# Four of the attention stage's eight modulation blocks computed on VectorE during the mixer's input projection, the other four at half a block per head

## The reference, cut to what matters

```
m_lat = split(silu(c) @ ada_w[i] + ada_b[i], 6)       # ada_w[i]: 2048 x 12288
h = x;  hn = rms_norm(h) * (1 + m_lat[1]) + m_lat[0]
layer 0: p = hn @ w_in                                 # 512 tokens x 6560 columns
         y = [diff_attention(p[:, :3072]), rwkv7(p[:, 3072:])] @ w_out
layer 1: conformer convolution
h = h + m_lat[2] * y                                   # output gate of the mixer
h = h + m_lat[5] * mlp(rms_norm(h) * (1 + m_lat[4]) + m_lat[3])
```

## Time and profile before

| | us |
|---|---|
| median of 3 runs | 3243.42 |
| profiled execution, span from first to last instruction | 3244.1 |
| input projection, from its first matmul to its last copy | 121.8 to 606.5 |
| attention | 606.5 to about 740 |
| TensorE / VectorE / ScalarE busy | 3021.5 / 2202.5 / 1244.9 |

### The profile page before, as it was taken

How to read it: one execution, slowest core, us unless ns; L and a number is a source line. 1 busy time by engine, 2 the same in 40 slices (tenths; PEclk the granted TensorE clock), 3 DMA queues, 4 the chain that set the end, 5 groups by cost and what they waited for, 6 DMA issues and landing times.

```text
span 3244.1 us, 49985 instructions
## 1 busy us (share of the span) xinstructions
PE 3021.5 (93%) x20896; PEld 2496.8 (77%) x20896; DVE 2202.5 (68%) x2736; ACT 1244.9 (38%) x1430; POOL 217.1 (7%) x394
## 2 busy tenths in 40 slices
PE   5899999778889888999999999999889999999999
PEld 2588987536677766788888888799867888888887
DVE  3677766477887885577777878759974555555554
ACT  1322221174444443344443434343643343434342
POOL 1000000001000000012122121100000000000000
PEclk9799999899999998999999999999989999999999
DMA  9976887790000033668888888756205455555553
GB/s 326 352 273 238 317 289 246 271 368 24 12 14 13 22 67 106 208 230 285 279 295 281 293 292 277 260 166 184 92 23 181 159 194 186 191 185 192 194 182 130
DMA packets 306013, 640.59 MB, mean 197 GB/s; under 512 B 19035, under 2 KB 23937, under 8 KB 303585
## 3 DMA queue, kind: packets, MB, share of 16 engines
q1 hardware_dynamic: 269280, 529.94, 48.3%
q0 software_dynamic: 28384, 94.76, 9.0%
q10 hardware_dynamic: 8128, 12.72, 1.1%
HBM read 623.81 MB, written 13.40 MB: 196 GB/s over the span
## 4 chain that ended last, share of the span: by engine, by line
PE 83%; DVE 9%; DMA 4%; issue 2%; ACT 2%; ACTq 0%; SPq 0%; POOLq 0%; DVEq 0%
PE ps L445 46%; PE ps L463 15%; PE ps L465 7%; DMA raw<-in_ada_w_dram 3%; PE ps L2385 2%; PE ps L1662 2%; DVE rw_scl L1336 1%; DVE rw_mb L1353 1%; PE ps L382 1%; PE ps L1820 1%; PE ps L1772 1%; DVE rw_mt L1356 1%; DVE rw_scc L1339 1%; PE ps L1569 1%; DVE line L752 1%
## 5 line engine op out<-in xcount | busy, mean ns | idle before, releaser
L422 DVE TENSOR_TENSOR split_lo<-raw,split_hi 128x2048 fp32r<-128x2048 f32 (+1 forms) x372 | 849.7, 2285 | 496.7 <-ACT split_hi L410 488.8
L410 ACT ACTIVATE split_hi<-raw 128x2048 fp32r<-128x2048 f32 x368 | 702.1, 1911 | 1180.4 <-PE ps L445 840.3
L463 PE MATMUL ps<-xa,split_hi 128*128 128x512 f32 x2048 | 723.4, 398 | 6.4 <-ACT xa L617 6.4
L465 PE MATMUL ps<-xa,split_lo 128*128 128x256 f32 x2048 | 574.0, 280 | 0.0
L463 PEld LDWEIGHTS ps<-xa,split_hi 128*128 128x128 f32 x2048 | 384.6, 188 | 103.0 <-ACT xa L617 7.4
L445 PE MATMUL ps<-split_hi,hT_hi 128*128 128x512 f32 x1024 | 399.6, 390 | 0.0
L445 PE MATMUL ps<-split_hi,hT_lo 128*128 128x512 f32 x1024 | 398.5, 389 | 0.0
L445 PE MATMUL ps<-split_lo,hT_hi 128*128 128x512 f32 x1024 | 398.4, 389 | 0.0
L465 PEld LDWEIGHTS ps<-xa,split_lo 128*128 128x128 f32 x2048 | 386.5, 189 | 0.2
L445 PEld LDWEIGHTS ps<-split_hi,hT_hi 128*128 128x128 f32 x1024 | 192.2, 188 | 41.4 <-issue 1.8
L445 PEld LDWEIGHTS ps<-split_hi,hT_lo 128*128 128x128 f32 x1024 | 192.2, 188 | 40.2
(11 more groups left out here) (386 smaller groups left out, 4521.1 us busy)
## 6 DMA issues: line engine op xcount, KB each, us to landing
raw<-in_mlp_w_dram SPq DMA_DIRECT2D x256, 1024.0 KB, 5.4
raw<-in_ada_w_dram SPq DMA_DIRECT2D x64, 1024.0 KB, 9.6
raw<-in_mix_in_w_dram SPq DMA_DIRECT2D x48, 1024.0 KB, 5.7
raw<-in_conv_pw_w_dram SPq DMA_DIRECT2D x48, 1024.0 KB, 5.4
gate<-in_ada_w_dram SPq DMA_DIRECT2D x172, 256.0 KB, 5.0
line<-in_ada_w_dram POOLq DMA_DIRECT2D x171, 256.0 KB, 5.1
late<-in_ada_w_dram POOLq DMA_DIRECT2D x85, 256.0 KB, 5.0
tmpa<-in_ada_w_dram SPq DMA_DIRECT2D x84, 256.0 KB, 4.9
```

What stands on the lines that cost most here:

```text
L410: nc.scalar.activation(split_hi[:, c, :, 0:n], raw[:, c, :, 0:n], ACT.Copy).then_inc(hi_done, 1)
L422: nc.vector.tensor_tensor(split_lo[:, c, :, 0:n], raw[:, c, :, 0:n], split_hi[:, c, :, 0:n], ALU.subtract).then_inc(lo_done, 1)
L463: pe.matmul(ps[:, base + j, :], split_hi[:, c, kk, j * P:(j + 1) * P], both, start=(k == 0), stop=False, skip_group_check=True)
L465: mm = pe.matmul(ps[:, base + j, 0:SEQ], split_lo[:, c, kk, j * P:(j + 1) * P], xa_hi[:, k, :], start=False, stop=(k == KT - 1), skip_grou ...
```

## The change

The output gate's blocks 8 to 11 are made on VectorE beside the projection (20 blocks, 320 pieces instead of 256), with other rates per item. The attention keeps blocks 12 to 15: two chunks per head, a block over two heads, and a copy and store on ScalarE in every second head. The gate is now stored as one row, so it is read with one DMA instead of four, behind another semaphore.

```diff
-ADA_A, ADA_T = 8, 1
-ADA_M, M_BUF = 16, 6
+ADA_A, ADA_T = 8, 4
+ADA_M, M_BUF = 20, 6
 Q_AT = ADA_A
-Q_ALL = Q_AT + ADA_T * HEADS
+Q_ALL = Q_AT + ADA_T
-        PARTED = [(0, 2), (0, 3)]
+        PARTED = [(0, 3)]
             if n == 0:
-                pool.wait_ge(ada_st, 16 * 4)
+                pool.wait_ge(mrow_st, 16 * ADA_M)
         def mix_ada(b):
-            return (0, (16 + b) * NB) if b < 8 else (1, (b - 8) * NB)
+            if b < 8:
+                return 0, (16 + b) * NB
+            return (1, (b - 8) * NB) if b < 16 else (0, (b - 8) * NB)
-        STEP_RATE = [3, 1, 7, 4, 4, 8, 3, 3, 7, 7, 7, 8, 8]
+        STEP_RATE = [3, 1, 8, 6, 6, 9, 8, 8, 8, 8, 9, 9, 0]
             gate_bias(pool, 0, 2)
-            for g in range(4):
+            for g in range(parts_of(0, 2)):
                 gate_part(pool, 0, 0, 2, g)
-            pool.wait_ge(ada_st, 16 * HEADS)
+            pool.wait_ge(ada_st, 16 * ADA_T)
-            with sp.Fori(0, HEADS) as i:
-                q = i + Q_AT
-                send_ada(sp, 0, i * NB + Q_AT * NB, ("ada", q - 1))
+            for i in range(ADA_T):
+                send_ada(sp, 0, (16 - ADA_T + i) * NB, ("ada", Q_AT + i - 1))
-                    if n < HEADS:
-                        act_ada(act, 0, (n + Q_AT) * NB, n + Q_AT, 0, n * 16, 0)
+                    if n < HEADS and n % 2:
+                        i = n // 2
+                        act_ada(act, 0, (16 - ADA_T + i) * NB, i + Q_AT, 0, i * 16, 0)
-            def weights(i, c):
-
+            def weights(n, half):
+
+                i, c = n // 2, 2 * (n % 2) + half
                 pe_ada_chunk(pe, i + Q_AT, i + (Q_AT + MIX_M), c, 0, i + Q_AT)
                     if n < HEADS:
                         weights(n, 0)
-                        weights(n, 1)
                     if n:
                         maps_turned(n - 1)
                     if n < HEADS:
-                        weights(n, 2)
+                        weights(n, 1)
                     if n + 1 < HEADS:
                         turned(n + 1)
-                    if n < HEADS:
-                        weights(n, 3)
```

## The result

The kernel after takes 3271.57 us (median of 4 runs, 3270.39 to 3274.56) against 3244.06 us before (median of 4, 3241.31 to 3245.73): ratio 1.0088, 95% interval 1.0073 to 1.0102. It is slower by 27.5 us; 3260 was forecast, with 3250 to 3270 as the forecast's own range and 3243 to 3277 as the whole one. Its profiled execution has a span of 3268.7 us and took 3270.39 us, so the spans differ by 24.6 us, and the traces have to explain that number. (Wherever both are on record, the time exceeds the span by about 1.7 us, so the span of 3244.1 before fits its run of 3245.73 us, the slowest of the four, while the one after is its fastest: that is the 3 us between the two differences.)

The account below looks back on a forecast made before the run. TensorE was taken as the bound, with 83% of the chain, and VectorE's lead as used up in product 7. Projection +30 and attention -13.3 gave +16.7, 3260 us; own range 3250 to 3270, 8-in-10 range 3243 to 3277.

Parts of the forecast that it names:

- rival 3: Projection: piece waits of 2.0 to 2.3 us in every item, +36 to +44 instead of +30, 3266 to 3274; chance 0.13.
- The item sum: Projection, products 5 to 7: VectorE's split 2.2 us, steps, and piece wait per item, added without pause from 315.3 to 443.8.
- The step that ends the twelfth block: Projection, product 7: VectorE's step at 443.8, needed by the sum before chunk (8,2), which starts 29.6 us later.
- The restart after the last stall: Projection: TensorE restarts slowly after a stall, 1.3 us each; only the last counts, +1.4.
- The small stalls of before: Projection: the stall at 548.82 and a like one in product 12 go, estimated -2 us.
- -0.9 as forecast: Attention: one head's wait for a chunk before its values goes, 0.6 us and part of the chunk's 1.06.
- Heads 0 to 2: Attention: the 6.86 us chunk wait goes and 22.5 us between maxima becomes an ordinary head's 11.9, -10.6.
- "Thus no gain" in an ordinary head: Attention: the 11.9 us chain from one head's values to the next holds no transfer, so nothing is gained.
- rival 2: Attention: 2.7 us gaps drop TensorE to half clock, values 4.0 instead of 2.0 us in eight heads, +16, 3276; chance 0.09.
- Head 6's -1.8: Attention, head 6: the 3.74 us wait stays, but one of two chunks that cost 3.46 us goes, -1.8.
- 4 (it costs nothing): Projection: moved blocks cost TensorE nothing and the attention gains as forecast, -13, 3230; chance 0.06.
- rival 1: VectorE's lead covers products 6 and 7; transfer-paced attention heads speed up to -23.5: net -8.5, 3235; chance 0.12.

Follow-up runs that it names:

- the other rates: Kernel after with the same 320 steps at other rates per product, 4 and 6 in products 6 and 7: 3262.35 us, ratio 1.0051 to the kernel before.
- one buffer more: Kernel after with seven piece buffers instead of six: 3265.81 us, ratio 1.0069 to the kernel before.
- the second table version: Kernel after with ScalarE's square-root wait in every second head moved behind the wait for the next maxima: 3267.70 us, ratio 1.0073 to the kernel before.
- one round of filler: Kernel after, first table edit (no effect in the targeted heads), plus four zero-adding matmuls in heads 1 to 7 before the second half block: 3272.29 us, ratio 1.0077.
- attention alone: Kernel after with the projection's old 16 blocks and rates, blocks 8 to 11 left out: 3241.18 us, ratio 0.998 to the kernel before.
- two rounds: Kernel after with seven buffers, other rates, freed table load, and twice four zero-adding matmuls in heads 1 to 7: 3247.45 us, ratio 1.0007 to the kernel before.

## Why the prediction was right, and where it was off

The direction was right and the time lies in the range, but the size was short: +16.7 forecast, +24.6 in the spans, +27.5 in the medians. The 3271.6 us lie outside of the forecast's own 3250 to 3270, and by the number alone rival 3 (3266 to 3274) would have had it; what speaks for the forecast's mechanism is the projection, walked step by step below. Nearly the whole miss is one term.

**The projection, +30 forecast, +28.8 measured.** Its steps hold one by one:
- Product 5's first split at 315.3 forecast, 315.31 measured. Product 6's at 364.9 and 363.59, product 7's at 408.2 and 406.34. The item sum (split, steps, a piece wait) was good to 2 us over 93.
- The step that ends the twelfth block: 443.8 forecast; the sum that needs it starts at 441.32, so chunk (8,2) follows at about 441.9, 27.7 us later than before (29.6 forecast).
- Two waits of 15 and 8 us were expected. There are three: 3.79 ahead of (7,1), 11.40 ahead of (7,2) and 6.42 ahead of (8,2). Places and total are nearly as said (21.6 against 23).
- The restart after the last stall cost 3.1 us instead of 1.4: the two chunks in the earlier trace rows, from which the 1.4 was taken, had got full clock back sooner. The small stalls of before were 1.6 us where 2 was estimated. 27.7 + 3.1 - 1.6 = 29.2, 0.4 over the measured 28.8; the further 1 us of stalls in products 8 to 11 did not come, for no later sum waits.
- That the agreement is to 1 us is luck. The six kernels with this projection end it between 631.5 and 639.6 and the three with the old one between 604.8 and 606.5, so a pair of executions can give 25 to 35 us; the means differ by 29.5.
- That the place of the steps matters, and not their number alone, is shown by the other rates: same steps, 10 us less. Rival 3 took longer piece waits for the cause: the waits in the seven items of products 6 and 7 ahead of the deadline were 1.0 to 1.9 us, 1.3 on average (1.1 forecast), and one buffer more nearly halves all piece waits and moves TensorE's by 2.5 us, so they are not the main part.

**The attention, -13.3 forecast, -5.2 measured.** This is the term that was mis-sized. From the start of one head's values to that of the next, the difference between the two kernels closes:

| stretch | after minus before, us | of it |
|---|---|---|
| end of the projection to head 0's values | -9.5 | -10.6 forecast |
| head 1's values to head 2's | +2.6 | table load 0.6, the rest half clock |
| head 3's to head 4's | -0.3 | -0.9 as forecast, table load 0.6 |
| head 4's to head 5's | +0.1 | -1.8 forecast |
| head 5's to head 6's | +0.6 | table load 0.6 |
| head 6's to head 7's | +0.9 | half clock |
| the rest | +0.4 | |

- Heads 0 to 2: -10.6 forecast, -9.5 measured. Right but for 1.1 us, of which half clock in head 1's scores (3.02 us instead of 1.99, behind 3.70 us of idle) would account for 1.0.
- "Thus no gain" in an ordinary head was too kind: three of them lose. A table load became exposed in heads 3, 5 and 7. In the kernel before, every such head had ScalarE's copy of the sums (act_ada) between the root and the exponential, and the table load came early behind it. Without that copy the wait for the maxima goes to the table load. That the copy had taken up the wait for the root is my reading of this. I had priced ScalarE's removed copies at nothing because they stood in idle time; what they did for the order of waits I did not see. Shown by the second table version: 0.6 us in each of the three steps, 1.8 in all. With the load freed, the ordinary head is 11.9 us as forecast, and head 4 has its -0.9 (11.21 us against 12.10), though this is not firm: the same step took 11.23 and 11.83 us in two other executions of the old attention.
- The clock was charged at nothing, and that was wrong. After gaps of 2.79 and 3.84 us the values ran at half clock: the values of head 1 and the scores behind them lost 1.7 + 1.8 us, the values of head 6 1.1, of which 2.0 and 0.9 show in the steps to the next head. My ground was one row of before, 2.42 us of idle and no fall, and one row was too little: in the kernel before with a seventh buffer, whose attention is the same, the same gap was followed by half clock.

```profile
719.12 3.50 PE L2904 MATMUL ps<-at_v,at_pT 128*128 128x128 f32 x16 [2.42 <-DVE at_pT L2748]
```

The Trainium skill (TensorE: Matmul & The Clock Gate, "Why this matters for your kernels") warns of idle gaps between bursts of matmuls above a length that it gives, after which the array falls back to half rate. The clock fell here after shorter gaps too (2.79 us, and 1.90 with one round of filler), so the measurement decides. This was rival 2, with 0.09 and +16, and the prediction's own list of what would show it wrong has half-clock values; it came in part, on top of the forecast, not in its place.
- Head 6's -1.8 did not come: of two chunks at half clock one went, but the half clock now lasted longer. From the first half block to the values it is 5.63 us (5.51 before): half block, transposes and half block took 1.93, 1.97 and 1.94 us, where before the transposes and the last chunk took 1.20 and 1.07. With the second table version, where the last of them took 1.06, the stretch gained 0.9.

Which gap costs the clock differs from execution to execution, and with it the size of this term: attention alone, which has the half clock in four heads, gained only 1.2 us there.

**The rest.** The recurrence and what follows are unchanged (0.6 us in 524), as said. Of the rivals, 1 (VectorE's lead covers it) and 4 (it costs nothing) fell by the three stalls. The other half of rival 1, heads paced by transfers, fell too: the DMA engines' share in the attention went from 0.88 to 0.55 and an ordinary head kept its 11.9 us.

## What to carry to other kernels

Work moved to an engine that is idle on average is paid where that engine has no lead: walk its items one by one through the densest stretch, and find the first thing that the bottleneck needs from it. With item times from the trace, that sum came out within 2 us of the one execution measured, in a stretch that varies by 8; and moving steps ahead of the dense stretch took back a third of the loss.

An instruction in idle time isn't free to remove: ask what waits it took up, and what follows it in order. And work taken from the bottleneck's gaps is worth less than its length where what remains then runs at half clock.

## What the hardware showed that I had not expected

- A gap's length alone doesn't settle whether TensorE's clock falls. With the second table version, values after 2.75 us of idle took 2.02 us, and the next head's, after 2.76, took 3.28. With one round of filler it fell after a gap of 1.90 (2.84 us), and with two rounds, at gaps of at most 1.55, it did not fall. Nor does the program decide: ahead of head 1's values the kernel after idled 2.79 us and they took 3.75 us; with seven buffers or other rates they took 2.02 us after 2.79 and 2.76.

```profile
671.57 2.02 PE L2907 MATMUL ps<-at_v,at_pT 128*128 128x128 f32 x16 [2.75 <-DVE at_pT L2750]
683.46 3.28 PE L2907 MATMUL ps<-at_v,at_pT 128*128 128x128 f32 x16 [2.76 <-DVE at_pT L2750]
```

- The order in which the program states its waits decided here which of two adjacent instructions, the table load or the exponential, carried them. With the waits stated as maxima, root, map, the table load (1.28 us) starts early; with root, maxima, map it starts after the maxima.
- After a stall of 6.42 us, TensorE ran 6.2 us at half clock with back-to-back matmuls before it was granted full clock. The stalls of 3.79 and 11.40 us were followed by 3.4 and 4.7 us at half clock, so the longest stall did not have the longest restart. A stall on a matmul-bound path costs more than its own length: three stalls of 21.6 us came with about 7.2 us lost to half clock.
